# Weights that stay are loaded from ScalarE's queue, and the tile mixed next is projected last, straight from PSUM

## What is computed

```python
def layer(x, ...):
    h = rmsnorm(x, norm_mix_w)
    proj = h @ w_in                                   # 1024 -> 2824 columns
    ... = split(proj)                                 # mLSTM q, k, v, o, gates; attention q, k, v
    hm = sigmoid(mo) * head_rmsnorm(mlstm_scan(...))  # 4 heads of 128, a state carried from row to row
    hs = swa(...)                                     # 8 heads, window 128
    x = x + concatenate([hm, hs]) @ w_out             # 1024 x 1024
    h2 = rmsnorm(x, norm_ffn_w)
    x = x + peer(h2, w_q, keys_1, keys_2, peer_u, peer_v)
    return x

def peer(x, w_q, ...):
    q = x @ w_q                                       # 1024 -> 8 heads x 256
    s1, s2 = q1 @ keys_1.T, q2 @ keys_2.T             # 128 scores each
    idx, top = best 16 of the 16 x 16 sums            # of 16384 experts
    g = softmax(top)
    a = gelu(sum_d(peer_u[idx] * x))
    return sum_k(g * a * peer_v[idx])
```

## Time and profile before

| | us |
|---|---|
| median of 3 runs | 3286.49 |
| lowest, highest | 3281.36, 3294.59 |
| the profiled execution, as timed | 3287.95 |
| its span, first to last instruction | 3286.2 |

### The profile page before, as it was taken

How to read it: one execution, slowest core, us unless ns; L and a number is a source line. 1 busy time by engine, 2 the same in 40 slices (tenths; PEclk the granted TensorE clock), 3 DMA queues, 4 the chain that set the end, 5 groups by cost and what they waited for, 6 DMA issues and landing times.

```text
span 3286.2 us, 34549 instructions
## 1 busy us (share of the span) xinstructions
PE 2585.3 (79%) x11351; PEld 1055.1 (32%) x11351; DVE 2079.2 (63%) x5202; ACT 580.3 (18%) x1057; POOL 1995.7 (61%) x2128
## 2 busy tenths in 40 slices
PE   8995886788769899947967786778767886789666
PEld 4562352235224433313522242234222341125111
DVE  1246677776776467637657776777677667765653
ACT  2211111211121212112112111211122111210111
POOL 0015576767765466636567676777676676755775
PEclk9996897789788999968888897789878887775878
DMA  6079999999999999998899999999999999988998
GB/s 243 26 267 403 344 376 405 396 364 407 409 386 379 344 407 407 373 384 316 330 361 408 396 401 407 399 398 403 407 409 384 366 407 399 406 337 296 394 405 331
DMA packets 351818, 1206.27 MB, mean 367 GB/s; under 512 B 37840, under 2 KB 55128, under 8 KB 349592
## 3 DMA queue, kind: packets, MB, share of 16 engines
q0 software_dynamic: 304128, 1107.43, 86.3%
q1 hardware_dynamic: 47512, 96.64, 7.9%
HBM read 1188.42 MB, written 15.60 MB: 366 GB/s over the span
## 4 chain that ended last, share of the span: by engine, by line
PE 40%; DMA 23%; DVE 13%; POOL 10%; issue 6%; DVEq 4%; ACT 2%; SPq 1%; ACTq 1%; POOLq 0%
DMA ring<-in_peer_u_dram,idx 13%; PE acc L1502 12%; DMA ring<-in_peer_v_dram,idx 7%; DVE ring L1141 7%; PE mx L1397 6%; POOL ring L529 5%; POOL ring L518 5%; PE mx L1382 4%; PE acc L1213 4%; PE acc L1462 3%; PE mx L1228 3%; DVEq L1045 2%; PE h2p L1437 2%; PE acc L1448 2%; DMA proj_scratch<-weights 1%
## 5 line engine op out<-in xcount | busy, mean ns | idle before, releaser
L1502 PE MATMUL acc<-ring,wk 128*32 128x512 f32 x4224 | 1259.6, 729 | 474.8 <-DMA ring<-in_peer_v_dram,idx 436.1
L1141 DVE SCALAR_TENSOR_TENSOR ring<-ring,h2p 128x1024 f32<-128x1024 f32 x1056 | 1281.0, 1216 | 556.1 <-DMA ring<-in_peer_u_dram,idx 466.5
L518 POOL DMA_INDIRECT ring<-in_peer_u_dram,idx x1056 | 997.1, 944 | 720.5 <-DVE ring L1141 264.9
L529 POOL DMA_INDIRECT ring<-in_peer_v_dram,idx x1056 | 996.5, 944 | 550.8 <-issue 273.6
L1502 PEld LDWEIGHTS acc<-ring,wk 128*32 128x32 f32 x4224 | 252.5, 123 | 1305.6 <-issue 1233.1
L1397 PEld LDWEIGHTS mx<-reg,weights 128*128 128x128 f32 x2048 | 249.9, 202 | 73.5 <-issue 73.5
L1397 PE MATMUL mx<-reg,weights 128*128 128x128 f32 (+1 forms) x2048 | 263.7, 288 | 2.0 <-DVEq L1024 1.3
L1462 PE MATMUL acc<-xt,ident 32*32 32x512 f32 x132 | 100.1, 899 | 94.1 <-DVEq L1110 94.1
L721 ACT ACTIVATE gl<-dots 128x16 f32<-128x16 f32 x66 | 14.2, 216 | 702.7 <-DVEq L1144 702.6
L1437 PE MATMUL h2p<-ch,ident 32*32 32x512 f32 x528 | 86.3, 780 | 55.6 <-DVEq L1144 55.6
L1382 PE MATMUL mx<-weights,reg 128*128 128x512 f32 (+1 forms) x256 | 128.2, 655 | 0.0
(11 more groups left out here) (279 smaller groups left out, 2339.6 us busy)
## 6 DMA issues: line engine op xcount, KB each, us to landing
weights<-in_w_in_dram SPq DMA_DIRECT2D x10, 2048.0 KB, 18.9
ring<-in_peer_u_dram,idx POOLq DMA_INDIRECT x1056, 8.1
ring<-in_peer_v_dram,idx POOLq DMA_INDIRECT x1056, 8.0
weights<-in_peer_w_q_dram SPq DMA_DIRECT2D x8, 2048.0 KB, 26.9
ring<-in_peer_w_q_dram SPq DMA_DIRECT2D x8, 1024.0 KB, 5.7
weights<-in_w_out_dram SPq DMA_DIRECT2D x2, 4096.0 KB, 23.5
proj_scratch<-weights SPq DMA_DIRECT2D x20, 256.0 KB, 6.1
pj<-proj_scratch SPq DMA_DIRECT2D x7, 644.0 KB, 13.9
```

Of the source, the lines that this page charges most:

```text
L518: pool.indirect_dma_start(ring[:, n % NU, :], None, u_d, bass.IndirectOffsetOnAxis(ap=idx[:, g % 4, k:k + 1], axis=0)).then_inc(u_in[n % N ...
L529: pool.indirect_dma_start(ring[:, NU + n % NV, :], None, v_d, bass.IndirectOffsetOnAxis(ap=idx[:, g % 4, k:k + 1], axis=0)).then_inc(v_in[ ...
L1141: V.scalar_tensor_tensor(ring[:, n % NU, :], ring[:, n % NU, :], 1.0, h2p[:, :], ALU.mult, ALU.mult, accum_out=dots[:, (g + 1) % 2, k:k + ...
L1502: last = T.matmul(acc[j:j + SUB, cols], wk[:, g % 2, i, :], ring[:, NU + (TOPK * g + i) % NV, cols], start=not own and g % 2 == 0 and i == ...
```

## The change

**Queue.** The first load of w_out and w_q moves from SP to ACT's queue (`load_weights`): w_out and the first quarter behind ACT's copy of chunk 2 of tile 3, two quarters behind that of chunk 4, the last at the end of the group. SP keeps the stores alone there.

**Order.** Tiles 4 to 8 are projected in the order 5, 6, 7, sample, 4 (`ORDER`). The sample takes slots 360 to 366, tile 4 slots 368 to 390. Tile 4's chunks are copied straight into `pj` and `vx` (`first`), so it has neither stores nor a `load_p`, only the rotation table.

**Second load of the weights.** SP issues it after the sample's six stores: w_out when chunk 1 of tile 4 is ready, one quarter of w_q with each of chunks 2 to 5.

**Table.** Tile 4's mixing starts at 390 instead of 396, at the same density. For all tiles the steps from `residual` to `h2_copy` move 3 later in r, `query` and `query_copy` 2, `score_keys` 1.

```diff
+ORDER = [0, 1, 2, 3, 5, 6, 7, SAMPLE, FIRST]
+AT_S, AT_LAST = TILES - 2, TILES - 1
...
-PE_AT += [("out_proj", i, 58 + i // 2) for i in range(8)] + [("h2_transpose", 0, 69)]
-PE_AT += [("query", i, 73 + i) for i in range(16)] + [("score_keys", i, 90 + i) for i in range(4)]
+PE_AT += [("out_proj", i, 58 + i // 2) for i in range(8)] + [("h2_transpose", 0, 72)]
+PE_AT += [("query", i, 75 + i) for i in range(16)] + [("score_keys", i, 91 + i) for i in range(4)]
...
-        return 396 + r * 60 // 100
+        return 390 + r * 60 // 100
...
-    return AGAIN + 2 * (((m - FIRST) * NC_ + c) * 2 + half)
+    return AGAIN + 2 * (((n - FIRST) * NC_ + c) * 2 + half) - (2 * 2 * (NC_ - 2) if n == AT_LAST else 0)
...
+def copies_until(n):
+    return 3 * n if n <= AT_S else 3 * (n - 1) + 1
+def p_landed(m):
+    return 64 * m if m < FIRST else 64 * (m - 1) + 16
...
             def load_p(m):
...
+                if m == FIRST:
+                    sp.dma_start(rot[0:n, :], rot_tab[r:r + n, :]).then_inc(p_in, 16)
+                    return
...
-                sp.wait_ge(chunk_ready, NC_ * SAMPLE + 1)
-                load_wout()
-                load_wq(0)
-                load_wq(2)
-                sp.wait_ge(chunk_act, 3 * SAMPLE + 1)
+                load_x1_again(AT_LAST)
+                sp.wait_ge(chunk_act, copies_until(AT_S) + 1)
                 for c, (c0, w) in enumerate(PC):
                     if c == 4:
-                        sp.wait_ge(chunk_dve, 3 * SAMPLE + 1)
-                        load_wq(4)
+                        sp.wait_ge(chunk_dve, copies_until(AT_S) + 1)
                     q = c % 4 * SUB
                     sp.dma_start(proj_d[0:DEC, c0:c0 + w], po_again[q:q + SUB, 0:w]).then_inc(po_out, 16)
-                sp.wait_ge(po_out, 16 * NC_ * (TILES - FIRST))
-                load_wq(6)
+                for c in range(1, NC_):
+                    sp.wait_ge(chunk_ready, chunks_until(AT_LAST) + c + 1)
+                    if c == 1:
+                        load_wout()
+                    else:
+                        if c == NC_ - 1:
+                            sp.wait_ge(po_out, 16 * NC_ * (TILES - 1 - FIRST))
+                        load_wq(2 * (c - 2))
...
             for c in range(1, NC_):
-                sp.wait_ge(chunk_ready, NC_ * (FIRST - 1) + c + 1)
-                if c == 1:
-                    load_wout()
-                else:
-                    load_wq(2 * (c - 2))
                 store_proj(FIRST - 1, c)
...
             def chunk_copy(m, c):
...
+                if m == AT_LAST:
+                    if c == 2:
+                        S.activation(first[c], pbank_again[c].rearrange("p (h e) -> p h e", h=MH), ACT.Copy, scale=scale)
+                    else:
+                        S.activation(first[c], pbank_again[c], ACT.Copy, scale=scale)
...
+            def load_weights(c):
+                act.wait_ge(chunk_ready, NC_ * (FIRST - 1) + c + 1)
+                if c == 2:
+                    act.dma_start(wout_s, w_out[0].rearrange("(k p) c -> p k c", p=P)).then_inc(wout_in, 16)
+                for k in {2: (0,), 4: (2, 4), 5: (6,)}[c]:
+                    act.dma_start(wq_s[:, k:k + 2, :], w_q[0, k * P:(k + 2) * P, :].rearrange("(k p) c -> p k c", p=P)).then_inc(wq_in, 16)
...
                     if g < 0 and k in LAST_ACT:
                         chunk_copy(FIRST - 1, LAST_ACT[k])
+                        load_weights(LAST_ACT[k])
+                    if g < 0 and k == TOPK - 1:
+                        load_weights(NC_ - 1)
...
-                        dve.wait_ge(p_in, 64 * m)
+                        dve.wait_ge(p_in, p_landed(m))
+                        if m == FIRST:
+                            dve.wait_ge(chunk_act, copies_until(TILES))
```

More of the change, by code:

```diff
@@ L69 @@
           ("softmax_max", 0, 39), ("softmax_max", 1, 40), ("softmax_args", 0, 41), ("softmax_sum", 0, 46), ("probs_copy", 0, 48),
[L70 removed]
+          ("concat", 0, 52), ("finish", 0, 53), ("cat_copy", 0, 56), ("residual", 0, 66), ("normalise", 0, 70), ("h2_copy", 0, 74)]
 EARLY_END = 57
@@ L781, in _ @@
                         hT1_copy(FIRST)
[L782 to L789 removed]
+                    for n in range(FIRST, TILES):
+                        if n < AT_LAST and t == project_at(n, 1, 0):
+                            rms1(n + 1)
+                        if n < AT_LAST and t == project_at(n, 4 if n < AT_S else 1, 0) + 1:
+                            hT1_copy(n + 1)
+                        for c in range(0, NC_ if n != AT_S else 1, 2):
+                            if t == project_at(n, c, 1) + 1:
+                                chunk_copy(n, c)
                     if t == window(SAMPLE) + 2:
@@ L829, in chunk_copy @@
             def chunk_copy(m, c):
-                dve.wait_ge(chunk_ready, NC_ * m + c + 1)
+                dve.wait_ge(chunk_ready, chunks_until(m) + c + 1)
                 rinv = nr1[:, m % 2, 2:3]
-                if m >= FIRST:
+                if m == AT_LAST:
+                    V.tensor_scalar(first[c], pbank_again[c], rinv, None, ALU.mult)
+                elif m >= FIRST:
                     dve.wait_ge(po_out, 16 * (NC_ * (m - FIRST) + c))
@@ L1509, in _ @@
                         transpose1(FIRST)
-                    for m in range(FIRST, TILES):
-                        for c in range(NC_ if m < SAMPLE else 2):
+                    for n in range(FIRST, TILES):
+                        for c in range(NC_ if n != AT_S else 2):
                             for half in range(2):
-                                if t == project_at(m, c, half):
-                                    if c == 4 and half == 0:
-                                        transpose1(m + 1)
-                                    project_again(m, c, half)
+                                if t == project_at(n, c, half):
+                                    if n < AT_LAST and c == (4 if n < AT_S else 1) and half == 0:
+                                        transpose1(n + 1)
+                                    project_again(n, c, half)
                     if t == window(SAMPLE) + 1:
```

86 lines of the change are left out of this document (41 added, 45 removed).

## The result

The changed kernel took 3277.7 us (median of 17 runs, 3261.8 to 3289.1) beside 3294.6 us for the kernel before on the same chip: a ratio of 0.9948, 95% interval 0.993 to 0.9967, or 17 us less where 33 were forecast. Run again twice beside the kernel before, it gave 0.9908 (0.9876 to 0.994) and 0.9927 (0.9902 to 0.9952). The differences of the medians are -17, -26 and -22 us. The time is inside the forecast's range and the mechanisms forecast for tile 4 are there, but 7 to 16 of the 33 us are missing. The question is where they went.

A forecast was written before the change was run, and what follows sets the result against it. DMA engines were taken as the bound, losing time only where the data rate falls. Terms -7.1, -(2 + 4 + 5 + 7 + 2), -8 and +2 gave -33 us, 3254 us as a median; range 3234 to 3284.

The forecast's parts named there:

- Bytes: Tile 4's projection no longer goes out and back, 2.89 MB less for the DMA engines: -7.1 us.
- tail: Projection's end and second weight load: sample's stores precede the weights, shrinking DVE's 33.2 us wait; 2 us gained, bounds 0 and 9.
- scores: Tile 4's attention scores move ahead of a PE row sum, easing DVE's 13.3 us wait: 5 us gained, bounds 0 and 11.
- residual: Tile 4's w_out and residual: the later step cuts DVE's 15.1 us wait to about 7; 7 us gained, bounds 0 and 12.
- queries: Tile 4's queries start two slots later against w_out, bound by PE: 2 us gained, bounds -3 and 5.
- the rival of the bytes alone: Tile 4's mixing is bound by PE's density, so only the saved traffic counts: 3281 us, chance 0.20.
- The signs named: Right: DVE's sample-store wait under 8 us, tile 4's first chunk to scores over 370 GB/s; wrong: first gathers under 350.
- The rotation table: Tile 4's table has fewer loads ahead of it, shortening DVE's 16.8 us wait: 4 us gained, bounds 0 and 6.
- The rival of the table behind the weights: Tile 4's rotation table still lands some 22 us after issue, DVE waits 10 us or more: 3260 us, chance 0.09.
- The other tiles: Seven tiles besides 0 and 4: later residual removes DVE's w_out waits, 1.1 us a tile, -8 us, bounds 0 and -20.
- Half clock: PE runs at 1.2 GHz beside the weights in the projection's tail, delaying tile 4's mixing: 3313 us, chance 0.07.
- The first load: First weight load from ACT's queue: w_out starts 8 us later, costing +2 us, bounds -2 and +8.

The follow-up runs named there:

- root ahead: The changed kernel with the norm's square root at r = 66 instead of 68: 3264.8 us, 0.991 on a quick chip; 0.9888 on a slower one.
- order alone: The kernel before with the new projection order, tile 4 straight from PSUM, the later second weight load and mixing from slot 390: 3278.5 us, 0.9959.
- table first: The changed kernel with the norm's square root at r = 66 and tile 4's rotation table issued before the second weight load: 3266.0 us, 0.9905.
- tables alone: The kernel before with only the new step tables, two runs on slower chips: 1.0006 and 0.9994.
- old places in tiles 5 to 7: The changed kernel with tiles 5 to 7 using the earlier places in r of the mixing steps: 3277.5 us, 0.9941.
- queue alone: The kernel before with only the first load of w_out and w_q moved to ACT's queue, two runs on slower chips: 1.0004 and 0.9984.

## Why the prediction was half right

*Bytes*: 1206.27 MB became 1203.38, the 2.89 forecast.

*The block around tile 4* (bytes, tail, table, scores, residual, queries): forecast -27. Measured by profiles: 367.4 (366.9 in the second) became 345.7, 342.9 and 348.2, so -19 to -25, and -26 with root ahead. The sum was nearly right and its split was not, so part of its being right is luck: slots 360 to 400 gave 17.4 us and 400 to 464 only 4.4, where the terms put 13 (bytes among them) and 14. DVE's wait for the residual fell to 7.8 as forecast ("about 7"). With the order alone slots 400 to 464 take 213.7 us, 5 more than before; with the tables (and the queue) they take 204.5. Three stretches after, from 12 us before the weights' first issue to the table, then to the scores and to the residual:

```profile
1350.00:1437.00 87.00, 66.13 (x196) 21.42 (x194) 42.83 (x104) 11.66 (x17) 43.96 (x47) 0.89 1.02 406
1437.00:1500.00 63.00, 46.92 (x183) 18.44 (x185) 42.79 (x119) 16.98 (x34) 37.75 (x40) 0.75 0.93 354
1500.00:1555.00 55.00, 46.33 (x190) 20.33 (x188) 35.96 (x86) 9.43 (x26) 27.17 (x29) 0.88 0.89 324
```

The stretch with the weights runs at 406 GB/s, and from the scores to the residual it is 324. Between the same two waits the kernel before had 301:

```profile
1541.50:1594.00 52.50, 47.46 (x194) 23.64 (x194) 31.55 (x74) 7.41 (x24) 26.22 (x28) 0.84 0.81 301
```

That is better but far from 408, with PE busy 46.3 of 55 us. PE's density as the limit that remains, which the rival of the bytes alone named, fits this; no run changed the density.

*The signs named.* DVE's wait for the sample's stores is 9.0 us, not under 8. From tile 4's first chunk (1341) to its scores the rate is 375 GB/s, over the 370 named, but the kernel before had 366 there, so that sign tells little. The first 50 us of gathers run at 352 GB/s, just over the 350 that was to show an error, and without a loss (below).

*The rotation table* was called right in its wait, 7.6 instead of 16.8, with 13.0 us instead of 22.4 from its issue to DVE's next instruction. That the rest of the wait is covered shows in table first. The rival of the table behind the weights (22 us to land) did not come. What the shorter wait itself was worth no run shows.

*The other tiles, -8, and the clock in tiles 5 to 7, put at nothing*: here the prediction failed, in one term of the sum and in one that the sum lacks. The term took a wait of DVE for w_out as lost data rate, at 1.1 us a tile. The waits went (100.1 to 37.3) and hardly any time followed: tables alone gave 1.0006 and 0.9994, and the old places in tiles 5 to 7 left that stretch as long (1209.8 us beside 1211.7). The stretch at w_out of tile 5 ran at 401 GB/s *with* its wait of 5.4 us. The prediction had the measure at hand, a wait is worth what the data rate loses beside it, and applied it to three of the nine waits and took one figure for all seven tiles. It also took 1.24 slots for a step of r in all of them, where tile 3 has 0.60. Nothing at all would be too strong: around tile 8's w_out (slots 912 to 940) the three profiles with the old places take 86.4 to 87.2 us and the seven with the new ones 77.3 to 82.2. But most of that is given back by slot 1039: from 912 on it is 367, 362 and 362 us in the changed kernel and 368 and 364 before.

The missing term is PE's clock after a short idle time. In the profiles of the changed kernel tiles 5 to 7 took 6 to 17 us more, with the late return to 2.4 GHz as the part that can be seen. "Half clock" was a rival, but placed in the projection's tail, where the clock was 0.89 from 1350 to 1437; I did not ask where else PE comes back from a short idle time into dense work. Whether the change causes it is open, as said above.

*The first load, +2*: on the quick chip slots -16 to 0 took 44.7 us instead of 46.8, and queue alone gave 1.0004 and 0.9984. On slower chips that stretch is longer with the queue (51.8 to 53.6 us) than without (50.0 to 52.2), and by slot 256 there is no difference. So 0. w_out was issued at 232.86, the 8 us later that were foreseen, and it cost nothing that can be seen. POOL's waits for the stores, the 16.0 us among them, are gone from its list, and were covered too. The Trainium skill, "DMA: Bandwidth & Descriptors", "Issuing engines are not separate DMA queues", agrees: another issuer gave no bandwidth. By its "Queues, rings and completion order" the stores could still have been reported late; the trace shows no such wait: beside weights on another queue tile 3's stores of 256 KB landed 7.7 us after their issue, where it was 24.8 behind weights on the same queue (medians of three).

*In sum*: forecast -33 without the failed -8 and without the +2 is -27. The profiles put +6 to +17 on it in tiles 5 to 7, and between -6 and +3 in the last tile, depending on which profile of the kernel before stands beside: -27 to -7. The medians say -17, -26 and -22. So the account fits, but it is too wide to prove itself: slots 0 to 360 alone vary by 15 us between two profiles of the kernel before, as much as the part in question.

## What to carry to other kernels

Price a wait by the data rate of its own stretch, every one of them: 63 us of waits went here, and outside the block around tile 4 no gain from them can be told from the noise. Where a table moves a step behind another on a slow engine, look what that other waits for: three places in r put a root behind 14 us of waiting. Where an engine's clock falls with a short idle time, list the places where dense work follows one; a few of them, early in one execution and late in another, weigh as much as the edit. Before subtracting two profiles, set each profiled execution beside the median of its kernel.

## What the runs showed of the hardware

The same kernel took 3294 us on some chips and 3605 to 3626 on others. A free-running stretch of 123 us moves 409 GB/s in the changed kernel on a quick chip and 361 in queue alone on a slower one:

```profile
1657.30:1780.30 123.00, 84.68 (x315) 26.23 (x313) 94.89 (x249) 22.57 (x43) 87.41 (x94) 0.84 1.03 409
```

```profile
1830.50:1953.50 123.00, 76.75 (x276) 22.16 (x277) 90.17 (x243) 22.57 (x43) 80.87 (x85) 0.77 0.96 361
```

On the slower chips the kernels with the new order came to 0.9876 to 0.9924 of the kernel before, on quick chips those of the changed kernel and its variants to 0.9905 to 0.9959. On the slower chips PE did not idle for the gather ahead of w_out (2.8 us at most, 4.5 in tiles 5 and 6 of most profiles of quick chips), and the same 32 matmuls took 7.5 us, all at 2.4 GHz, in tiles 5 to 7 of all ten profiles.

Two executions of the kernel before differ by 13 us, 9.6 of them in slots 256 to 288. First profile, then second:

```profile
979.80:1101.30 121.50, 105.64 (x628) 56.30 (x624) 64.37 (x153) 22.93 (x35) 64.56 (x69) 0.85 0.98 378
1008.90:1045.90 37.00, 32.56 (x96) 13.27 (x96) 16.30 (x35) 4.22 (x6) 15.88 (x18) 0.77 0.93 356
```

```profile
975.80:1087.70 111.90, 98.05 (x630) 53.72 (x626) 64.22 (x152) 22.87 (x35) 63.85 (x68) 0.91 1.03 406
1003.00:1040.00 37.00, 33.23 (x136) 13.91 (x134) 21.28 (x49) 4.81 (x7) 20.39 (x22) 0.94 1.03 405
```

It looks like the same event: TensorE's clock is 0.77 in the one and 0.94 in the other, and the data rate 356 and 405 GB/s. The kernel is the same, so here it is a draw of the execution. A few such places of 5 to 10 us each could make up the spread of a kernel's runs (25 of the kernel before from 3281 to 3312 us), and they let a single profile mislead by that much.
